# Modulation units and silu(c) moved forward, softmax scaling on ScalarE, one bank for cross scores

## What is computed

```
# first block: mixer = sliding attention (8 heads) and mLSTM (4 heads), then cross attention, then a gated FFN
h = rmsnorm(x, norm_mix_g);  p = h @ w_in          # columns aq, akv, mqk, mv, mo and the gates
s = aq @ ak.T * 64**-0.5 - slope * dist            # window of 128
p_ = exp(s - m);  p_ = p_ / (sum(p_) + exp(sink - m));  attn_out = p_ @ av
mqk = silu(causal_conv4(p[mqk]));  mlstm_out = sigmoid(mo) * mlstm(mqk, mv, gates)
x = x + concat(attn_out, mlstm_out) @ w_out
x = x + softmax((rmsnorm(x) @ wq) @ (rmsnorm(mem) @ wk).T / 16) @ (rmsnorm(mem) @ wv) @ wo   # 4 heads of 256
x = x + (silu(conv3(u1)) * u2) @ w_down            # u = rmsnorm(x) @ w_up
# second block: two layers, each modulated by c
mod = silu(c) @ w_ada + b_ada                      # 2 x 3072 and 2048 values: shift, scale, gate
x = x + gate * gdn(modulated_norm(x));  x = x + gate * stick_breaking_attention(modulated_norm(x), kv)
```

## Time and profile before

| | |
|---|---|
| median of three runs | 927.01 us (926.12 to 929.07) |
| the profiled execution | 927.45 us, span 925.5 us |
| PE busy | 836.0 us (90%), 7056 matmuls |
| PEld busy | 771.6 us (83%) |
| DVE busy | 648.3 us (70%), 1320 instructions |
| ACT busy | 494.4 us (53%), 997 instructions |
| DMA | 148.49 MB, mean 160 GB/s |
| chain of work that ended last | PE 66%, DVE 22%, ACT 9%, issue 2%, DMA 1% |

### The profile page before, as it was taken

The page is one execution under the profiler, slowest core; times in us unless marked ns, Lnnn a source line. Parts: engine busy times, 40 slices in busy tenths (PEclk is TensorE's granted clock), DMA queues, the critical chain, the costliest instruction groups (busy, mean ns, idle before and its releaser), DMA issues.

```text
span 925.5 us, 16890 instructions
## 1 busy us (share of the span) xinstructions
PE 836.0 (90%) x7056; PEld 771.6 (83%) x7056; DVE 648.3 (70%) x1320; ACT 494.4 (53%) x997; POOL 0.2 (0%) x4
## 2 busy tenths in 40 slices
PE   3987999989898999999978899999988879999998
PEld 3876898989888999999967687878776868988888
DVE  5489967996668898888767776666553888543454
ACT  4564553453436666665546635454762457467762
POOL 0000000000000000000000000000000000000000
PEclk9999899999989999999998999999996999999999
DMA  9513663665336565546671421212120556621311
GB/s 343 229 47 136 236 266 137 233 268 210 146 104 228 193 238 200 204 143 234 258 304 51 177 93 46 83 56 79 61 101 37 186 193 258 232 109 70 137 46 46
DMA packets 22684, 148.49 MB, mean 160 GB/s; under 512 B 2641, under 2 KB 3025, under 8 KB 6481
## 3 DMA queue, kind: packets, MB, share of 16 engines
q1 hardware_dynamic: 22608, 147.43, 43.3%
HBM read 146.37 MB, written 1.05 MB: 159 GB/s over the span
## 4 chain that ended last, share of the span: by engine, by line
PE 66%; DVE 22%; ACT 9%; issue 2%; DMA 1%; SPq 0%; DVEq 0%; ACTq 0%
PE ps L1925 49%; DVE wlo L1426 4%; DVE raw L1448 4%; ACT L1019 1%; DVE vt L1423 1%; DVE kT L1423 1%; PE ps L2239 1%; DVE tmp L1423 1%; PE ps L2090 1%; ACT whi L1040 1%; DVE mqk L1423 1%; DVE p0lo L1426 1%; PE ps L2131 1%; PE ps L2149 1%; PE ps L2159 1%
## 5 line engine op out<-in xcount | busy, mean ns | idle before, releaser
L1925 PE MATMUL ps<-p0hi,whi 128*128 128x256 f32 x1128 | 330.7, 293 | 18.9 <-DVE wlo L1426 6.5
L1925 PE MATMUL ps<-p0lo,whi 128*128 128x256 f32 x1128 | 318.6, 282 | 0.0
L1925 PE MATMUL ps<-p0hi,wlo 128*128 128x256 f32 x1128 | 318.5, 282 | 0.0
L1426 DVE TENSOR_TENSOR wlo<-raw,whi 128x512 fp32r<-128x512 f32 (+2 forms) x436 | 271.8, 659 | 20.0 <-ACT whi L1040 19.6
L1040 ACT ACTIVATE whi<-raw 128x512 fp32r<-128x512 f32 (+2 forms) x436 | 237.8, 599 | 10.0 <-DMA raw<-wst 10.0
L1925 PEld LDWEIGHTS ps<-p0hi,whi 128*128 128x128 f32 x1128 | 216.1, 192 | 30.7 <-issue 20.4
L1925 PEld LDWEIGHTS ps<-p0lo,whi 128*128 128x128 f32 x1128 | 216.2, 192 | 1.0 <-issue 0.8
L1925 PEld LDWEIGHTS ps<-p0hi,wlo 128*128 128x128 f32 x1128 | 215.9, 191 | 0.0
L1448 DVE CUSTOM_DVE_ANT_0 raw<-raw,cact,vc 128x1024 f32<-128x1024 f32 x64 | 79.5, 1279 | 0.0
L1925 PE MATMUL ps<-zhi,whi 128*128 128x256 f32 x176 | 49.4, 280 | 3.0 <-DVE wlo L1426 3.0
L1925 PE MATMUL ps<-zhi,wlo 128*128 128x256 f32 x176 | 48.9, 278 | 0.0
(11 more groups left out here) (352 smaller groups left out, 1430.2 us busy)
## 6 DMA issues: line engine op xcount, KB each, us to landing
raw<-wst SPq DMA_DIRECT2D x125, 1024.0 KB, 5.0
raw<-wsd SPq DMA_DIRECT2D x16, 704.0 KB, 4.8
x<-xT SPq DMA_DIRECT2D x4, 256.0 KB, 4.7
m_x<-memT SPq DMA_DIRECT2D x1, 1024.0 KB, 8.2
outT<-x SPq DMA_DIRECT2D x4, 256.0 KB, 2.4
cact<-cB SPq DMA_DIRECT2D x1, 512.0 KB, 13.9
cst<-con SPq DMA_DIRECT2D x1, 356.0 KB, 12.3
smo<-conr SPq DMA_DIRECT2D x1, 320.0 KB, 12.1
```

Of the source, the lines that this page charges most:

```text
L1426: return v.tensor_tensor(lo, src, hi.bitcast(F32), ALU.subtract)
L1925: ins = t.matmul(o, a, b, start=first and q == 0, stop=last and q == len(ops) - 1, skip_group_check=True)
```

## The change

It edits the planner's list and five steps.

- `unit_order`: the first six modulation units stand behind aq1, akv and the four mqk units, no longer behind mqk1 to mqk3, mv0, mv1 and mo0. Those from the seventh on stay in place.
- `csilu c` follows `aq(0)` and no longer `av`; the load of c is issued ahead of unit 2, now the first modulation unit.
- `w_norm` ends with the reciprocal. The two scalings become a new job `w_sc` on ACT behind each `w_norm`, two activations with the reciprocal as pointer scale; `w_tp` waits for `w_sc`.
- `gain_steps("x")`: a step of the units ahead of xq is taken behind each group, as long as there are any.
- `cross`: both blocks' scores go to one bank. One `c_max` over both, `c_exp` twice, then a yield, then one `c_norm`: one reciprocal and two scalings. `c_qk(h)` waits for `c_cp(h-2)` alone, `c_tp(h)` for `c_norm(h)` and `c_ptc(h-2)`.

```diff
@@ -129,11 +129,11 @@
...
 
-    add("aq", 0, 2)
-    add("akv", 0)
-    mixed("mqk", 0, 4, (1, 2, 3))
-    mixed("mv", 0, 2, (0, 1))
-    mixed("mo", 0, 2, (0,))
+    mixed("aq", 0, 2, (1,))
+    mixed("akv", 0, 1, (0,))
+    mixed("mqk", 0, 4, (0, 1, 2, 3))
+    add("mv", 0, 2)
+    add("mo", 0, 2)
@@ -398,10 +398,14 @@
...
             add("av")
-            add("csilu", "c")
+
+        def on_aq(i):
+            add("aq", i)
+            if i == 0:
+                add("csilu", "c")
...
         self.handler.update(
-            aq=lambda i: add("aq", i), akv=on_akv, mqk=on_mqk, mv=lambda i: add("mv", i),
+            aq=on_aq, akv=on_akv, mqk=on_mqk, mv=lambda i: add("mv", i),
@@ -442,6 +446,7 @@
...
                 add("w_norm", j, hh)
+                add("w_sc", j, hh)
@@ -486,23 +491,24 @@
...
         self.run_to(self.at("xv", 1))
+        self.limit = self.at("xq")
...
         for _ in self.gain_steps("x"):
-            pass
+            if self.unit < self.at("xq"):
+                self.step()
...
             yield
-            for b in range(2):
-                add("c_qk", h, b)
-                add("c_max", h, b)
-                add("c_exp", h, b)
-                add("c_norm", h, b)
-            yield
+            add("c_qk", h)
+            add("c_max", h)
+            add("c_exp", h)
+            yield
+            add("c_norm", h)
@@ -988,7 +994,7 @@
...
                     load("g", g2[:, :], wg2)
-                if k == 4:
+                if k == 2:
@@ -1249,6 +1255,13 @@
...
                     act.activation(sm[:, o + 6:o + 8], sm[:, o + 2:o + 4], ACT.Exp, bias=V("sink", j + 4 * hh)).then_inc(*tick("w_exp"))
+                elif kind == "w_sc":
+                    j, hh = i
+                    s2 = tr[3 * (j % 2) + hh]
+                    o = (j % 3 * 2 + hh) * 12
+                    e.wait_ge(*on("w_norm", j, hh))
+                    act.activation(s2[:, 0:P], s2[:, 0:P], ACT.Copy, scale=sm[:, o + 10:o + 11])
+                    act.activation(s2[:, P:384], s2[:, P:384], ACT.Copy, scale=sm[:, o + 11:o + 12]).then_inc(*tick("w_sc"))
@@ -1286,15 +1299,18 @@
...
                 elif kind == "c_exp":
+                    h, = i
+                    slot = h % 2
+                    o = slot * 24
                     lnexp()
-                    h, b = i
-                    slot = h % 2
-                    o = (slot * 2 + b) * 12
-                    e.wait_ge(*on("c_max", h, b))
+                    e.wait_ge(*on("c_max", h))
...
                         e.wait_ge(*on("c_tp", h - 2))
-                    act.activation(tr[3 * slot + b][:, 0:T], ps[3 + 2 * slot + b][:, 0:T], ACT.Exp, bias=sm[:, o + 1:o + 2],
-                                   accum_out=sm[:, o + 2:o + 3]).then_inc(*tick("c_exp"))
+                    for b in range(2):
+                        hb = slice(b * T, (b + 1) * T)
+                        ins = act.activation(tr[3 * slot][:, hb], ps[4 + 2 * slot][:, hb], ACT.Exp, bias=sm[:, o + 2 + b:o + 3 + b],
+                                             accum_out=sm[:, o + 4 + b:o + 5 + b])
+                    ins.then_inc(*tick("c_exp"))
@@ -1694,15 +1710,11 @@
...
                 elif kind == "w_norm":
                     j, hh = i
-                    s2 = tr[3 * (j % 2) + hh]
...
                     e.wait_ge(*own.last)
-                    own.mark(v.reciprocal(sm[:, o + 10:o + 12], sm[:, o + 8:o + 10]))
-                    e.wait_ge(*own.last)
-                    v.tensor_scalar(s2[:, 0:P], s2[:, 0:P], sm[:, o + 10:o + 11], None, ALU.mult)
-                    v.tensor_scalar(s2[:, P:384], s2[:, P:384], sm[:, o + 11:o + 12], None, ALU.mult).then_inc(*tick("w_norm"))
+                    v.reciprocal(sm[:, o + 10:o + 12], sm[:, o + 8:o + 10]).then_inc(*tick("w_norm"))
@@ -1735,20 +1747,21 @@
...
                 elif kind == "c_max":
-                    h, b = i
-                    o = (h % 2 * 2 + b) * 12
-                    e.wait_ge(*on("c_qk", h, b))
-                    own.mark(v.reduce_max(sm[:, o:o + 1], ps[3 + 2 * (h % 2) + b][:, 0:T], AX))
-                    e.wait_ge(*own.last)
-                    v.tensor_scalar(sm[:, o + 1:o + 2], sm[:, o:o + 1], -1.0, None, ALU.mult).then_inc(*tick("c_max"))
+                    h, = i
+                    o = h % 2 * 24
+                    e.wait_ge(*on("c_qk", h))
+                    own.mark(v.reduce_max(sm[:, o:o + 2], ps[4 + 2 * (h % 2)].rearrange("p (b t) -> p b t", b=2), AX))
+                    e.wait_ge(*own.last)
+                    v.tensor_scalar(sm[:, o + 2:o + 4], sm[:, o:o + 2], -1.0, None, ALU.mult).then_inc(*tick("c_max"))
                 elif kind == "c_norm":
-                    h, b = i
-                    o = (h % 2 * 2 + b) * 12
-                    s2 = tr[3 * (h % 2) + b][:, 0:T]
-                    e.wait_ge(*on("c_exp", h, b))
-                    own.mark(v.reciprocal(sm[:, o + 3:o + 4], sm[:, o + 2:o + 3]))
-                    e.wait_ge(*own.last)
-                    v.tensor_scalar(s2, s2, sm[:, o + 3:o + 4], None, ALU.mult).then_inc(*tick("c_norm"))
+                    h, = i
+                    o = h % 2 * 24
+                    s2 = tr[3 * (h % 2)]
+                    e.wait_ge(*on("c_exp", h))
+                    own.mark(v.reciprocal(sm[:, o + 6:o + 8], sm[:, o + 4:o + 6]))
+                    e.wait_ge(*own.last)
+                    v.tensor_scalar(s2[:, 0:T], s2[:, 0:T], sm[:, o + 6:o + 7], None, ALU.mult)
+                    v.tensor_scalar(s2[:, T:2 * T], s2[:, T:2 * T], sm[:, o + 7:o + 8], None, ALU.mult).then_inc(*tick("c_norm"))
@@ -2006,7 +2019,7 @@
                 elif kind == "w_tp":
...
                     slot = j % 2
-                    e.wait_ge(*on("w_norm", j, hh))
+                    e.wait_ge(*on("w_sc", j, hh))
@@ -2062,21 +2075,27 @@
...
                 elif kind == "c_qk":
-                    h, b = i
+                    h, = i
+                    bank = ps[4 + 2 * (h % 2)]
...
                     if h >= 2:
-                        e.wait_ge(*(on("c_cp", h - 2) if b else on("c_ptc", h - 2)))
-                    for c in range(2):
-                        ins = t.matmul(ps[3 + 2 * (h % 2) + b][:, 0:T], xq[:, 2 * h + c, b * P:(b + 1) * P], xk[:, 2 * h + c, :], start=c == 0, stop=c == 1)
+                        e.wait_ge(*on("c_cp", h - 2))
+                    for b in range(2):
+                        for c in range(2):
+                            ins = t.matmul(bank[:, b * T:(b + 1) * T], xq[:, 2 * h + c, b * P:(b + 1) * P], xk[:, 2 * h + c, :],
+                                           start=c == 0, stop=c == 1)
...
                 elif kind == "c_tp":
...
                     slot = h % 2
-                    e.wait_ge(*on("c_norm", h, 1))
+                    e.wait_ge(*on("c_norm", h))
+                    if h >= 2:
+                        e.wait_ge(*on("c_ptc", h - 2))
...
                         for m in range(2):
-                            ins = t.transpose(ps[3 + 2 * slot][:, m * T + b * P:m * T + (b + 1) * P], tr[3 * slot + b][:, m * P:(m + 1) * P], ident)
+                            ins = t.transpose(ps[3 + 2 * slot][:, m * T + b * P:m * T + (b + 1) * P],
+                                              tr[3 * slot][:, b * T + m * P:b * T + (m + 1) * P], ident)
```

More of the change, by code:

```diff
@@ L184 @@
     "w_qk": "win_pe", "w_tp": "win_pe", "w_av": "win_pe", "w_max": "win_dve", "w_norm": "win_dve",
-    "w_cp": "win_dve", "w_lo": "win_dve", "w_exp": "win_act", "w_ptc": "win_act", "w_hi": "win_act",
+    "w_cp": "win_dve", "w_lo": "win_dve", "w_exp": "win_act", "w_ptc": "win_act", "w_hi": "win_act", "w_sc": "win_act",
     "m_w": "mls_pe", "m_qk": "mls_pe", "m_et": "mls_pe", "m_nd": "mls_pe", "m_wexp": "mls_act",
```

## The result

In alternating runs the changed kernel took 933.12 us (median of 20) and the kernel before 928.57 (median of 20). The ratio is 1.0049, with a 95% interval from 1.0029 to 1.0069: slower by 4.5 us (2.7 to 6.4). Forecast were +3.85 us and 930.9 us; of the 2.2 us between 930.9 and 933.12, 1.6 are the kernel before, which came out at 928.57 and not 927.01 in these runs. The profiled execution of the changed kernel took 933.9 us (span 932.1), that of before 927.45.

A forecast was written before the change was run, and what follows sets the result against it. DVE and PE were taken to bound the edited first 262 us by turns, stage by stage. First stage 3.8, gate clock 1.6, norm x -1.85, head 1 -0.7 and head 3 1.0 give +3.85: 930.9 us, range 925 to 934.5.

The forecast's parts named there:

- Units: First stage: modulation units ahead of mqk0 and mqk1 cost +2.4 us each on DVE's chain; at the other places 0.
- Rival 2: First stage: DVE's idle times take the units in, so the kernel gets faster, -6 us, 921 us; chance 0.15.
- Low clock at the gates: PE's wait of 3.3 us ahead of its gate matmul brings the 1.2 GHz clock: +1.6 us, bounds 0 and +2.1.
- Pair 0 and 1: Sliding attention: pair 0 saves 1.1 us on DVE, shift +3.7; at pair 1 ACT adds 1.3, so PE gets +5.0.
- Pair 2 and 3: Sliding attention: pair 2 saves 1.1 us, leaving +3.8; pair 3 changes by 0.
- Norm x: Norm groups between parts of xv2: xq1 starts 1.85 us earlier; xq0 starts at once, some 1.6 us wait before xq1.
- Cross: Cross scores in one bank: head 1 -0.7 us, head 3 +1.0, heads 0 and 2 0 (up to +0.2 each).
- Clock at head 3: Low clock behind the wait in cross head 3 may last longer or shorter, -1.5 to +1.5 us; taken as 0.
- rival 3: PE's longer waits at 94.26 and 251.88 each bring 1.5 us more at low clock: +7, 934 us; chance 0.08.
- scalings on ScalarE: Sliding probabilities: moving w_norm's scalings off DVE saves 1.1 us a pair there; the move is worth 1.0 in the first stage.

The follow-up runs named there:

- e6: The changed kernel with 26 matmuls nobody reads filling TensorE's wait ahead of the gate matmul; ratio to the kernel before 1.0025.
- e11: The kernel before with units and silu(c) moved, and TensorE's waits ahead of the gate matmul and w_qk(2,0) filled with matmuls nobody reads; ratio 1.0030.
- e9: The changed kernel with one unit ahead of akv, none ahead of mqk0 and mqk1, the last behind mv1; ratio to the kernel before 1.0004.
- e1: The kernel before with only the modulation units and silu(c), with the load of c, moved; ratio 1.0084.
- e5: The kernel before with only the scalings of the sliding probabilities moved to ScalarE; ratio 1.0004.
- e3: The kernel before with only the norm groups and splits of norm x put between the parts of xv2; ratio 0.9955.
- e4: The kernel before with only the cross scores in one bank (one maximum, both exps, one norm); ratio 0.9986.
- e2: The changed kernel with the old order of the units and of silu(c); ratio to the kernel before 0.9987.
- e8: e7 with matmuls nobody reads filling TensorE's waits ahead of the transposes of gate rows, pair 3 and head 3; ratio to the kernel before 0.9920.
- e7: The changed kernel with old unit and silu(c) order except units from xv2 on one place later, pair 1's scalings on VectorE, head 3's norm directly behind its exps; ratio 0.9934.

## Why the prediction was right, step by step

The sign, the size and the mechanism held. The sum was +3.85; the trace shows +4.78, the timed runs +4.5. The sizes below are of one execution each, and the timed runs can't check them one by one.

- **Units.** Forecast +2.4 at the gates: e6 shows 2.33 without the low clock. Forecast +2.4 at the copy of pair 0: e11 has 4.77 for both. The unit and silu(c) ahead of akv cost nothing (e9). Rival 2, by which DVE's idle times take them in, is refuted by e1 and e11.
- **Low clock at the gates.** Forecast +1.6, measured 1.42 (3.75 less 2.33), behind a wait of 3.28 us. The low stretch is 6.8 us long, and PE's own loss in it is larger: the last part of mqk0 starts 3.2 us later than in e6 (shifts of 5.52 and 2.32). Of that 1.8 comes back at once, as the wait ahead of the transposes of the gate rows shrinks from 1.94 us before (1.95 in e6) to 0.17. The forecast counted only the gate matmul and w_qk(0,1), and not that PE would be slow for longer and then make it up at this wait, so there is some luck in how close it came.
- **Pair 0 and 1.** +3.7 and 1.6 of low clock make 5.3, measured 4.97. The sum over mem was to get 1.3 more through ACT: measured 6.33 less 4.97, 1.36; one w_sc takes 0.69 to 0.70 us in the chain, where 0.64 was taken. In e5 it is 0.93.
- **Pair 2 and 3.** -1.1 and 0 forecast, -0.95 and +0.10 measured. The wait ends at 100.76, or 99.9 with the start taken off.
- **Norm x.** -1.85 forecast, -1.73 measured (5.17 at the end of xv2 to 3.44), no wait ahead of xq0 and one of 1.43 ahead of xq1, forecast 1.6. That the 3.27 us ahead of xq0, which the chain gives as "issue", were DVE's order is shown by e3, where they are gone.
- **Cross.** Head 1: its wait is 0.57, forecast 0.6. Head 2 gave back 0.16, within the 0.2 named. Head 3: its wait went from 3.26 to 4.28, +1.02 where +1.0 was forecast.
- **Clock at head 3.** This is the term that was mis-sized. It was taken as 0 with bounds of 1.5 to each side; the low stretch is 10.2 us long instead of 6.8 and begins ahead of the transposes, which take 1.11 us here and 0.66 in e4. The length doesn't come from the edit: it is 10.2 in e1 and e11, which leave cross attention as it was, and 6.8 in e4. Head 3's part comes 1.38 later and not 1.02, and the next unit 0.33 more: +0.7 in all.

That is 0.7 of the 0.9 us by which the sum was short; the rest is spread. Of rival 3 this much came true: the stretch behind head 3's wait is longer. The one around pair 3's wait is 6.8 us as before.

Two steps were right for a reason that was only partly so. The scalings on ScalarE were to save 1.1 at pair 0. With the units in place DVE is late and the saving is real, but without them it is nothing (e2, e5). With the gate wait filled they are worth 4.77 (e11) less 3.55 (e6), 1.2 us, at pair 0, but at pair 3 only 4.76 less 4.24, 0.5 us, and not the 1.0 that the text gave; e6 has a short low stretch in between. And it was said that with the scalings left on DVE the units would cost 4.8: that is their DVE cost, but in e1 the wait of 2.41 us that this makes was followed by a low stretch of its own, and the last pair came 10.1 us later.

## What to carry to other kernels

Work put "where the engine is less busy" costs its full time if the place lies between a producer and the copy that the bounding engine waits for; ahead of akv the same unit was free, ahead of mqk0 it was 2.33 us and, in the trace of the change, 1.4 more of TensorE's clock. Look at each place for the next step on the chain, not at the share. A step moved to another engine lands in that engine's queue: name what stands behind it there. And in a change of several parts, try them one by one: norm x alone was 0.9955 and was hidden in a ratio of 1.0049.

## What was not expected of the hardware

**The same wait doesn't always bring the same clock.** Ten of the traces have the wait of 1.90 to 1.95 us ahead of the transposes of the gate rows, behind the same instructions but for the moved ones. Behind eight of them the granted clock falls to 0.50, for 3.4 us in seven and 6.8 in one; behind two (before and e6) it stays at 1.00. Sums of 54 to 58 us, before (first fence) and e2 (second), where the code is the same up to the scalings:

```profile
54.00:58.00 4.00, 3.28 (x22) 2.34 (x22) 3.79 (x13) 1.73 (x7) 0.00 (x0) 1.00 0.14 23
```
```profile
54.00:58.00 4.00, 4.00 (x20) 3.67 (x19) 3.79 (x12) 3.79 (x12) 0.00 (x0) 0.50 0.32 82
```

The wait of 3.07 to 3.27 us ahead of xq0 was accompanied by the low clock in four traces and not in e4, and the wait of 1.86 us at the start of up only in e8. What decides isn't seen in the rows. So one profiled execution against another carries a few us of this, and a step of 1 us has to be read from the starts around its place.

**Two paces at the full clock.** In the down stage, which no edit touches, the trace of before does 87 matmuls in 10 us and that of the change 91, both at a granted clock of 1.00 with PE full:

```profile
447.00:457.00 10.00, 10.00 (x87) 10.00 (x86) 7.59 (x18) 3.92 (x10) 0.00 (x0) 1.00 0.82 305
```
```profile
452.00:462.00 10.00, 10.00 (x91) 10.00 (x90) 8.09 (x18) 3.92 (x10) 0.00 (x0) 1.00 0.87 319
```

The cause stays open. Between 431 and 463 us of before the shift of the change's trace goes from +4.78 to +4.04, and that of e7's goes from -5.33 to -3.41 between 298 and 431 us, where the granted clock is 1.00 and PE full. That is another reason why the ends of two spans don't tell what an edit did.
